# A 16-row value block of attention padded with zeros to 128 rows

## The chip, the cores and the metric

The kernel runs on one core of a Trainium2 chip. The metric is the device time of one execution in microseconds (us). The core has five engines that run their own queues and meet only at semaphores: TensorE (PE, with its weight loads shown apart as PEld), VectorE (DVE), ScalarE (ACT), GpSimd (POOL) and SyncE (SP), which issues most of the DMAs here.

## The reference

Two layers of a model of width 1024 on 512 tokens, ahead of which 16 learned meta tokens are put, so T = 528. Each layer has a feed-forward part, a mixer and a second feed-forward part. One half of the mixer is causal attention with 8 heads, query and key width 96, value width 64:

```python
h = jnp.concatenate([meta, x], axis=1)            # 16 meta tokens, then 512
for l in range(DEPTH):                            # DEPTH = 2
    h = h + 0.5 * rms_norm(swiglu(rms_norm(h, ...), ...), ...)
    z = rms_norm(h, mix_pre_g[l]) @ w_in[l]
    xr, gr, cq, ckv, kr = jnp.split(z, splits, axis=-1)
    y_lru = rglru_group(xr, gr, ...)
    y_mla = mla_group(cq, ckv, kr, ...)           # attention
    y = concat(rms_norm(y_lru), rms_norm(y_mla)) @ w_out[l]
    h = h + rms_norm(y, mix_post_g[l])
    h = h + 0.5 * rms_norm(swiglu(rms_norm(h, ...), ...), ...)
return h[:, N_META:]
# attention, per head and block of 128 queries:
s = jnp.einsum('bqhd,bkhd->bhqk', q_blk, k) * scale
s = jnp.where(kpos[None, :] <= qpos[:, None], s, -jnp.inf)
o = jnp.einsum('bhqk,bkhd->bqhd', jax.nn.softmax(s), v)
```

## The kernel before

Activations stand feature by feature: 128 features on the partitions, 528 tokens along them. Every large product is made of three matmuls per tile (high part by high part, low by high, high by low), all in fp32r; the weight tiles run through a ring of four slots that SyncE loads, ScalarE copies to the high part (`hi`, L651) and GpSimd subtracts to the low part (`lo`, L590). This fills the feed-forward parts and the projections. The order of work on every engine is the order in which its block of the program is written; there is no scheduler.

The attention of a layer (`attention`, L1627) is written as a software pipeline over 32 items: item e is head e // 4 and query block i = e % 4 + 1. A query block has 128 queries, and sees keys 0 to 16 + 128 i. The keys are taken in blocks: block 0 is the 16 meta tokens alone, blocks 1 to 4 have 128 keys each (`block_of`, L519). Round e of the loop at L1710 puts on TensorE, in this order,

- `transposes(e - 2)`: i + 1 transposes of the exponentials `prob`, 128 columns each, L1691. That of block 0 turns keys 0 to 127, not only 16;
- `scores(e)`: query by keys, all columns, and one bf16 matmul `identb` by `maskb` that adds the causal mask to the last 128 columns (L1671, L1674);
- `outputs(e - 3)`: i + 1 pairs of a weight load of `probT` and a product with the value block `vt`, added up in one PSUM region (L1702 to L1705). For block 0 only rows 0 to 15 are read of both.

Since `mm` is a helper, the trace shows scores, mask and outputs all at L1372, and they are told apart by the names of their tiles: `kt,qt`, `maskb,identb` and `vt,probT`. A fp32 matmul shows as two records, so i + 1 products with `vt` are 2 (i + 1) records; the transposes are fp32 too but show one record each.

VectorE takes the row maximum of the scores (L1300), ScalarE the exponential with its row sum (L919), and the copy of the turned exponentials from PSUM to `probT` is ScalarE's for i of 1 and 2 (L970) and VectorE's for 3 and 4 (L1293). After the four blocks of a head VectorE scales the outputs (`head_out`, L1276 and L1277).

In the first layer the 16 meta tokens are queries too, in small matmuls of 16 by 16 (`meta_scores`, `meta_transposes`, `meta_outputs`); in the last layer they are left out, as nothing reads them.

The values come from three PSUM units, of 1024, 1024 and 512 columns: five blocks of 512 (8 heads by 64). Block 0's own product runs over tokens 0 to 127, so its rows 16 to 127 hold real values of other tokens, which no one reads. ScalarE copies the three units to `vt` (L872), ahead of a weight copy `hi` (L875) and the copies to `kt`.

Of the kernel before, what the change touches and what calls it, by code (L numbers as in the profile page):

```python
# [29 lines left out]
ACT = mybir.ActivationFunctionType  # L30
AX = mybir.AxisListType

P = 128
EPS = 1e-6
LRU_C = 8.0
N_META = 16
# [11 lines left out]
VD = 64  # L48
# [19 lines left out]
    NPAR += _n  # L68


C_ID, C_ONE, C_SEL, C_MASK, C_EPS, C_LNS, NCONST = 0, P, 2 * P, 3 * P, 4 * P, 4 * P + 1, 4 * P + 2


S_XR, S_CQ, S_GATE, S_CKV, S_KR, S_GR, S_V, S_K, S_Q, S_OUT = 0, 4, 7, 8, 10, 11, 15, 16, 17, 21
# [27 lines left out]
def build_program(nc, a, out, depth, d_ff):  # L102
# [64 lines left out]
    def slot_used(n):  # L167

        return n + 1 + RING
# [41 lines left out]
    with ExitStack() as ctx:  # L211
# [31 lines left out]
        consts = sb("consts", [P, NCONST], F32)  # L243
# [31 lines left out]
        vt = over("vt", [P, 5, HEADS * VD], F32, xch_at)  # L275
# [18 lines left out]
        probT = [over(f"probT{i}", [P, 5 * P], F32, z_at + 4 * CH + i * 5 * P * 4) for i in range(3)]  # L294
# [24 lines left out]
        def pair(i):  # L319
            return ps[:, i * 1024:(i + 1) * 1024]  # L320
# [3 lines left out]
        sel = consts[:, C_SEL:C_SEL + P]  # L324
        eps = consts[:, C_EPS:C_EPS + 1]
        ln_scale = consts[:, C_LNS:C_LNS + 1]

        def col(name, l, k, p=P):
            c = PCOL[name] + k
            return par[0:p, l, c:c + 1]  # L330
# [55 lines left out]
        psum_free = [sem(f"psum_free{i}") for i in range(4)]  # L386
# [132 lines left out]
        def block_of(j):  # L519

            return (0, N_META) if j == 0 else (N_META + (j - 1) * P, P)
# [109 lines left out]
        def _(act):  # L631
# [102 lines left out]
            def seam(b):  # L734
# [23 lines left out]
                if b < NB:  # L758
# [7 lines left out]
                                 scale=-1.0).then_inc(setup_exp, 1)  # L766
# [32 lines left out]
            def mixer(b):  # L799
# [10 lines left out]
                for g, dst in enumerate((rg, ig)):  # L810
                    for c in range(WC):
                        u = U[b, "gate"] + WC * g + c
# [3 lines left out]
                        else:  # L816
                            act.wait_ge(slots_used, slot_used(s0 + S_GATE))
                        nc.scalar.activation(halves(dst[:, c, :], False), unit(u, False), ACT.Tanh,
                                             scale=0.5, bias=half_b[:, l, g, c:c + 1])\
                            .then_inc(psum_free[pair_of(u)], 1)  # L820
                    hi(s0 + 10 + g)
                for c in range(QC):
                    u = U[b, "cq"] + c
                    act.wait_ge(psum_free[pair_of(u)], read_out(u))
                    nc.scalar.activation(cqh[:, c, :], cq[:, c, :], ACT.Copy,
                                         scale=col("mla_q_norm_g", l, c)).then_inc(cqh_ready, 1)

                for c in range(WC):
                    u = U[b, "gate"] + c
# [14 lines left out]
                for c in range(KVC):  # L844
                    act.wait_ge(ckvn_ready, KVC * l + c + 1)
                    nc.scalar.activation(ckvh[:, c, :], ckv[:, c, :], ACT.Copy,
                                         scale=col("mla_kv_norm_g", l, c)).then_inc(ckvh_ready, 1)
# [7 lines left out]
                for c in range(WC):  # L855
                    u = U[b, "gr"] + c
# [4 lines left out]
                u = U[b, "sel"]  # L861
                nc.scalar.activation(halves(tmp[0], False), unit(u, False), ACT.Copy)\
                    .then_inc(psum_free[pair_of(u)], 1)
                for i in range(3):
                    u = U[b, "v"] + i

                    if i < 2:
                        act.wait_ge(v_mm, 2 * l + i + 1)
                    else:
                        act.wait_ge(slots_used, slot_used(s0 + S_V))  # L870
                    n = 2 if i < 2 else 1
                    nc.scalar.activation(vt[:, 2 * i:2 * i + n, :],  # L872
                                         pair(pair_of(u)).rearrange("p (a b) -> p a b", a=2)[:, 0:n, :],
                                         ACT.Copy).then_inc(psum_free[pair_of(u)], 1)
                hi(s0 + 19)  # L875
                for i in range(HEADS // 2):
                    u = U[b, "k"] + i
# [16 lines left out]
                for c in range(WC):  # L894
                    act.wait_ge(yn_ready, WC * l + c + 1)
                    nc.scalar.activation(ylh[:, c, :], xc[:, c, :], ACT.Copy,
                                         scale=col("lru_out_g", l, c)).then_inc(ylh_ready, 1)
# [10 lines left out]
                for e in range(ITEMS + 2):  # L908
                    if e >= 2 and copied_by_act((e - 2) % NQ + 1):
                        transposed_copy_act(l, e - 2)  # L910
                    if e < ITEMS:
                        E, i = ITEMS * l + e, e % NQ + 1
# [12 lines left out]
                    i = e - (ITEMS - NQ)  # L925
# [18 lines left out]
                for i in range(NQ):  # L944
# [4 lines left out]
                                                scale=1.0 / W, bias=eps))  # L949
                nc.scalar.activation(small[:, 32:36], small[:, 32:36], ACT.Exp, scale=-0.5)\  # L950
                    .then_inc(rs_att, 1)
                for c in range(WC):
                    act.wait_ge(tr_mm, WC * l + c + 1)
                    pr, g = pair(pair_of(U[b, "tr"] + c)), col("mla_out_g", l, c)
                    if not trimmed(b):
                        nc.scalar.activation(xh[:, WC + c, 0:N_META], pr[:, 512:512 + N_META], ACT.Copy,
                                             scale=g)
# [402 lines left out]
        def _(pe):  # L1360
# [10 lines left out]
            def mm(o, w, x, start, stop):  # L1371
                return nc.tensor.matmul(o, w, x, start=start, stop=stop)  # L1372
# [254 lines left out]
            def attention(b):  # L1627
                l = b // 3

                last = U[b, "tr"] - 1  # L1630
                for u in range(last - 3, last + 1):
                    pe.wait_ge(psum_free[pair_of(u)], read_out(u))
                pe.wait_ge(krope_ready, 2 * (l + 1))
                m0, nm = n_meta_layers(l), N_META

                def meta_scores():
                    for hd in range(HEADS):
                        o = meta_turned(hd * nm, nm)  # L1640
                        mm(o, qt(hd)[:, 0:nm], kt(hd)[:, 0:nm], True, False)
                        ins = mm(o, identb[0:nm, 0:nm], maskb[0:nm, 0:nm], False, True)
                    ins.then_inc(s0_mm, 1)

                def meta_transposes():
                    pe.wait_ge(s0_exp, m0 + 1)
                    for hd in range(HEADS):

                        ins = mm(meta_turned(hd * nm, nm), prob[3][0:nm, hd * nm:(hd + 1) * nm],
                                 ident[0:nm, 0:nm], True, True)  # L1650
                    ins.then_inc(t0_mm, 1)

                def meta_outputs():
                    pe.wait_ge(t0_copied, 2 * m0 + 1)
                    for hd in range(HEADS):
                        ins = mm(ps[0:nm, 7 * 512 + hd * VD:7 * 512 + (hd + 1) * VD],
                                 probT[2][0:nm, hd * nm:(hd + 1) * nm],
                                 vt[0:nm, 0, hd * VD:(hd + 1) * VD], True, True)
                    ins.then_inc(o0_mm, 1)

                def scores(e):
                    E, hd, i = ITEMS * l + e, e // NQ, e % NQ + 1
                    t0, nk, c = block_of(i)[0], keys_of(i), place(e)
                    if before(e) is not None:
                        copied(before(e))
                    elif e == NQ and not trimmed(b):
                        pe.wait_ge(t0_copied, 2 * m0 + 1)
                    parts = [(0, nk, c)] if i < NQ else [(0, HALF, c), (HALF, HALF, c + 512)]
                    for k0, n, c0 in parts:
                        tail = k0 + n == nk  # L1670
                        mm(ps[:, c0:c0 + n], qt(hd)[:, t0:t0 + P], kt(hd)[:, k0:k0 + n], True, not tail)  # L1671
                        if tail:

                            ins = mm(ps[:, c0 + n - P:c0 + n], identb[:, :], maskb[:, :], False, True)  # L1674
                    ins.then_inc(s_mm, 1)

                def copied(e):

                    full, i = ITEMS // 2 * l + e // NQ * 2, e % NQ + 1
                    if copied_by_act(i):  # L1680
                        pe.wait_ge(t_act, full + i)
                    else:
                        pe.wait_ge(t_dve, full + i - 2)

                def transposes(e):
                    E, i = ITEMS * l + e, e % NQ + 1
                    pe.wait_ge(prob_ready, E + 1)
                    for j in range(i + 1):

                        k0, c0 = block_of(j)[0], place(e) + j * P  # L1690
                        ins = nc.tensor.transpose(ps[:, c0:c0 + P], prob[e % 4][:, k0:k0 + P], ident)  # L1691
                    ins.then_inc(t_mm, 1)

                def outputs(e):
                    hd, i = e // NQ, e % NQ + 1
                    copied(e)
                    if i == 1 and hd >= 2:
                        pe.wait_ge(o_copied, HEADS * l + hd - 1)
                    if e == NQ and not trimmed(b):
                        pe.wait_ge(t0_copied, 2 * m0 + 2)  # L1700
                    c0 = (hd % 2) * 512 + (i - 1) * VD
                    for j in range(i + 1):  # L1702
                        kn = block_of(j)[1]
                        ins = mm(pair(3)[:, c0:c0 + VD], probT[e % 3][0:kn, j * P:(j + 1) * P],
                                 vt[0:kn, j, hd * VD:(hd + 1) * VD], j == 0, j == i)  # L1705
                    ins.then_inc(pv_mm, 1)

                if not trimmed(b):
                    meta_scores()
                for e in range(ITEMS + 3):  # L1710
                    if e == 2 and not trimmed(b):
                        meta_transposes()
                    if 2 <= e < ITEMS + 2:
                        transposes(e - 2)
                    if e < ITEMS:
                        scores(e)
                    if e == 3 and not trimmed(b):
                        meta_outputs()
                    if e >= 3:
                        outputs(e - 3)  # L1720
# [36 lines left out]
def _consts():  # L1757
    c = np.zeros((P, NCONST), np.float32)
    c[:, C_ID:C_ID + P] = np.eye(P)
    c[:, C_ONE:C_ONE + P] = 1.0  # L1760
    for i in range(ROPE):
        for q in range(P // ROPE):
            c[i, C_SEL + q * ROPE + i] = 1.0
            c[ROPE + i, C_SEL + q * ROPE + i] = 1.0
    c[:, C_MASK:C_MASK + P] = np.triu(np.full((P, P), MASKED), 1)
    c[:, C_EPS] = EPS
    c[:, C_LNS] = -0.5 * np.log(NOPE + ROPE)
    return c

# [57 lines left out]
```

## Time and profile before

| | us |
|---|---|
| median of 3 executions | 2104.96 |
| lowest, highest | 2102.6, 2106.19 |
| the profiled execution | 2107.37 |
| its span, first to last instruction | 2105.5 |
| mean granted TensorE clock in it | 0.991 |

The span is 1.9 us shorter than its execution. In the rows below a line of a timeline gives the start in us, the time that the merged instructions cover, the engine, the line of the program, the operation, its output and inputs, their shapes, how many instructions are merged, and in brackets how long the engine sat idle before, and what ended that. `issue` stands for an idle time for which the profile shows nothing waited for. A shape such as `16*128` of a weight load is rows by columns of what is loaded into the array.

### The profile page before, as it was taken

The numbers are of one execution on the slowest core, as the hardware profiler recorded it, in microseconds if no ns is written. First come the engines' busy times: TensorE is split into PE (matmuls) and PEld (weight loads), VectorE is DVE, ScalarE is ACT, GpSimd is POOL, SyncE is SP. The second block draws the span as 40 slices with busy tenths as digits, with TensorE's granted clock in tenths as the row PEclk, the third lists the DMA queues.
The fourth block names the chain that finished last, engine by engine and source line by source line (L and its number), as shares of the span: only waits on it lengthen the run. The fifth ranks groups of instructions, "written<-read, shape, count | busy, mean of one in ns | idle before, by whom it ended". The sixth has DMA issues, their size and how long they took to land.

```text
span 2105.5 us, 39769 instructions
## 1 busy us (share of the span) xinstructions
PE 2062.0 (98%) x16488; PEld 2013.7 (96%) x16488; DVE 726.6 (35%) x1070; ACT 767.4 (36%) x1189; POOL 1057.1 (50%) x1280
## 2 busy tenths in 40 slices
PE   9999999999999999999999999999999999999998
PEld 8999999989889999999999999999898889999997
DVE  5222210468544322220062222104785453222102
ACT  5322232446545322332252222324455453332321
POOL 6655554566205655554375555545662156555542
PEclk9999999999999999999999999999999999999999
DMA  3222322122102222232222323221221013333322
GB/s 138 90 90 90 93 97 96 55 93 79 41 14 69 93 89 89 89 108 84 70 90 90 90 90 93 97 94 58 96 76 41 30 54 109 99 91 91 105 97 68
DMA packets 48274, 174.91 MB, mean 83 GB/s; under 512 B 5168, under 2 KB 9392, under 8 KB 48176
## 3 DMA queue, kind: packets, MB, share of 16 engines
q1 hardware_dynamic: 45792, 170.97, 25.6%
q10 hardware_dynamic: 2384, 2.52, 0.4%
q8 instruction: 75, 1.23, 0.2%
q14 instruction: 23, 0.19, 0.0%
HBM read 171.37 MB, written 2.10 MB: 82 GB/s over the span
## 4 chain that ended last, share of the span: by engine, by line
PE 85%; DVE 9%; POOL 2%; issue 2%; ACT 1%; DMA 1%; POOLq 0%; ACTq 0%; DVEq 0%; SPq 0%
PE ps L1372 83%; DVE xl L1046 2%; POOL wlo L590 1%; DVE h L1041 1%; PE ps L1691 1%; DVE xc L1137 1%; POOL tmp L623 1%; DVE tmp L1035 1%; DVE xcl L1145 0%; DVE ig L1158 0%; DVE xc L1160 0%; DVE cql L1152 0%; ACT xh L675 0%; DVE rg L1161 0%; DVE xc L1134 0%
## 5 line engine op out<-in xcount | busy, mean ns | idle before, releaser
L590 POOL TENSOR_TENSOR wlo<-raw,whi 128x256 fp32r<-128x256 f32 (+2 forms) x1192 | 991.1, 863 | 930.1 <-ACT whi L651 930.0
L1372 PE MATMUL ps<-xh,whi 128*128 128x264 f32 (+1 forms) x3392 | 727.3, 287 | 23.9 <-DVE xl L1046 18.0
L1372 PE MATMUL ps<-xl,whi 128*128 128x264 f32 (+1 forms) x3392 | 716.8, 284 | 0.0
L1372 PE MATMUL ps<-xh,wlo 128*128 128x264 f32 (+1 forms) x3392 | 716.0, 284 | 0.0
L1372 PEld LDWEIGHTS ps<-xh,whi 128*128 128x128 f32 x3392 | 538.7, 189 | 34.8 <-DVE xl L1046 24.0
L651 ACT ACTIVATE whi<-raw 128x1024 fp32r<-128x1024 f32 (+2 forms) x298 | 334.0, 1122 | 564.7 <-DMA raw<-in_ffn_down 263.1
L1372 PEld LDWEIGHTS ps<-xl,whi 128*128 128x128 f32 x3392 | 538.0, 189 | 0.8
L1372 PEld LDWEIGHTS ps<-xh,wlo 128*128 128x128 f32 x3392 | 537.5, 189 | 0.0
L1372 PE MATMUL ps<-hidh,whi 128*128 128x264 f32 (+1 forms) x1408 | 314.1, 284 | 0.0
L1372 PE MATMUL ps<-hidl,whi 128*128 128x264 f32 (+1 forms) x1408 | 312.9, 283 | 0.0
L1372 PE MATMUL ps<-hidh,wlo 128*128 128x264 f32 (+1 forms) x1408 | 312.9, 283 | 0.0
L1372 PEld LDWEIGHTS ps<-hidl,whi 128*128 128x128 f32 x1408 | 229.8, 188 | 0.1
L1372 PEld LDWEIGHTS ps<-hidh,wlo 128*128 128x128 f32 x1408 | 229.5, 188 | 0.0
L1372 PEld LDWEIGHTS ps<-hidh,whi 128*128 128x128 f32 x1408 | 229.0, 188 | 0.1
L1096 DVE TENSOR_TENSOR tmp<-ps,rs_in 128x528 f32<-128x528 f32 (+1 forms) x88 | 61.9, 704 | 407.4 <-PE ps L1372 407.4
L1075 DVE TENSOR_TENSOR tmp<-tmp,tmp 128x528 f32<-128x528 f32 (+3 forms) x44 | 42.0, 954 | 421.9 <-ACT tmp L706 387.2
L782 ACT ACTIVATE hidh<-tmp 128x528 f32 (+3 forms) x88 | 56.5, 642 | 228.6 <-DVE tmp L1100 228.6
L1093 DVE TENSOR_TENSOR tmp<-ps,rs_in 128x528 f32<-128x528 f32 (+1 forms) x88 | 61.9, 703 | 205.3 <-PE ps L1372 192.0
L779 ACT ACTIVATE tmp<-tmp 128x528 f32<-128x528 f32 (+1 forms) x88 | 56.6, 643 | 166.3 <-DVE tmp L1093 166.2
L1103 DVE TENSOR_TENSOR hidl<-tmp,hidh 128x528 f32 (+3 forms) x88 | 69.9, 794 | 80.6 <-ACT hidh L782 80.6
L623 POOL TENSOR_TENSOR tmp<-tmp,tmp 128x264 f32<-128x264 f32 (+1 forms) x66 | 52.6, 796 | 80.5 <-ACT tmp L680 76.7
L1046 DVE SCALAR_TENSOR_TENSOR xl<-h,par,xh 128x264 fp32r<-128x264 f32 (+1 forms) x96 | 76.5, 810 | 20.7 <-ACT xh L675 20.5
(174 smaller groups left out, 1556.0 us busy)
## 6 DMA issues: line engine op xcount, KB each, us to landing
raw<-in_ffn_gate SPq DMA_DIRECT2D x88, 512.0 KB, 3.5
raw<-in_ffn_up SPq DMA_DIRECT2D x88, 512.0 KB, 3.5
raw<-in_ffn_down SPq DMA_DIRECT2D x64, 704.0 KB, 4.0
raw<-in_w_in SPq DMA_DIRECT2D x28, 512.0 KB, 3.6
raw<-in_w_out SPq DMA_DIRECT2D x16, 512.0 KB, 3.5
raw<-in_w_q SPq DMA_DIRECT2D x8, 384.0 KB, 3.1
out_t<-h SPq DMA_DIRECT2D x16, 128.0 KB, 1.7
h<-in_x ACTq DMA_DIRECT2D x2, 528.0 KB, 8.5
```

The source lines that it names most:

```text
L590: ins = nc.gpsimd.tensor_tensor(wlo[:, r, at], raw[:, r, at], whi[:, r, at].bitcast(F32), ALU.subtract)
L623: nc.gpsimd.tensor_tensor(hs, hs, square_of(k, s, trim), ALU.add)\
L651: nc.scalar.activation(whi[:, r, 0:k], raw[:, r, 0:k], ACT.Copy).then_inc(hi_ready, 1)
L779: nc.scalar.activation(toks(tmp[2], trim), toks(tmp[0], trim), ACT.Silu).then_inc(silu_ready, 1)
L782: nc.scalar.activation(toks(hidh[:, mm, :], trim), toks(tmp[3], trim), ACT.Copy).then_inc(hidh_ready, 1)
L1035: nc.vector.tensor_tensor(scratch(k, s), half(f(b - 1, k), trim, s), bank(U[b, "post"], trim, s), ALU.mult).then_inc(step_ready, 1)
L1046: nc.vector.scalar_tensor_tensor(half(xl[:, k, :], trim, s), half(h[:, k, :], trim, s), col(g, l, k), half(xh[:, k, :], trim, s).bitcast(F32),
L1075: nc.vector.tensor_tensor(acc, acc, part(tmp[m % 2], trim), ALU.add).then_inc(sum_ready, 1)
L1093: nc.vector.tensor_tensor(halves(tmp[0], trim), unit(ug, trim), halves(rs_in, trim), ALU.mult).then_inc(psum_free[pair_of(ug)], 1)
L1096: nc.vector.tensor_tensor(halves(tmp[1], trim), unit(uu, trim), halves(rs_in, trim), ALU.mult).then_inc(psum_free[pair_of(uu)], 1)
L1103: nc.vector.tensor_tensor(toks(hidl[:, mm, :], trim), toks(tmp[3], trim), toks(hidh[:, mm, :], trim).bitcast(F32), ALU.subtract).then_inc( ...
L1372: return nc.tensor.matmul(o, w, x, start=start, stop=stop)
```

## The change

The copy of the first value unit is split in two. Block 0 is multiplied, on its way out of PSUM, by a new constant column that is 1 on rows 0 to 15 and 0 below; block 1 is copied as before. The products for block 0 then run over all 128 rows of `probT` and `vt`. The turned exponentials of keys 16 to 127 meet rows of zeros there, and these keys are counted once, in block 1, as before. The number and the order of TensorE's instructions stay as they are; ScalarE has one more instruction per layer. The small matmuls of the meta queries still read 16 rows.

```diff
+C_ID, C_ONE, C_SEL, C_MASK, C_EPS, C_LNS, C_META, NCONST = (
+    0, P, 2 * P, 3 * P, 4 * P, 4 * P + 1, 4 * P + 2, 4 * P + 3)
...
+        is_meta = consts[:, C_META:C_META + 1]
...
+                    if i == 0:
+                        nc.scalar.activation(vt[:, 0, :], pair(pair_of(u))[:, 0:512], ACT.Copy, scale=is_meta)
+                        nc.scalar.activation(vt[:, 1, :], pair(pair_of(u))[:, 512:1024],
+                                             ACT.Copy).then_inc(psum_free[pair_of(u)], 1)
+                        continue
                     n = 2 if i < 2 else 1
                     nc.scalar.activation(vt[:, 2 * i:2 * i + n, :],
...
                     for j in range(i + 1):
-                        kn = block_of(j)[1]
-                        ins = mm(pair(3)[:, c0:c0 + VD], probT[e % 3][0:kn, j * P:(j + 1) * P],
-                                 vt[0:kn, j, hd * VD:(hd + 1) * VD], j == 0, j == i)
+                        ins = mm(pair(3)[:, c0:c0 + VD], probT[e % 3][:, j * P:(j + 1) * P],
+                                 vt[:, j, hd * VD:(hd + 1) * VD], j == 0, j == i)
...
+    c[0:N_META, C_META] = 1.0
```

## Rows read from the trace of the kernel before

**Rows 1.** The page: busy time of the engines, and the chain that ended last
```profile
PE 2062.0 (98%) x16488; PEld 2013.7 (96%) x16488; DVE 726.6 (35%) x1070; ACT 767.4 (36%) x1189; POOL 1057.1 (50%) x1280
...
PE 85%; DVE 9%; POOL 2%; issue 2%; ACT 1%; DMA 1%; POOLq 0%; ACTq 0%; DVEq 0%; SPq 0%
```

**Rows 2.** Stretches: busy us of PE, PEld, DVE, ACT, POOL; granted clock; DMA share, GB/s
```profile
546.80:548.40 1.60, 1.60 (x5) 0.76 (x5) 0.00 (x0) 0.81 (x3) 1.50 (x3) 0.50 0.00 0
...
551.00:609.00 58.00, 58.00 (x402) 46.65 (x400) 28.93 (x58) 26.77 (x81) 2.78 (x4) 1.00 0.01 1
1600.00:1656.00 56.00, 56.00 (x382) 44.86 (x381) 27.55 (x55) 25.03 (x75) 4.09 (x6) 1.00 0.00 1
```

**Rows 3.** Timeline of TensorE's weight loads over one head, layer 1
```profile
559.92 0.66 PEld L1372 LDWEIGHTS ps<-vt,probT 16*128 16x128 f32 x4 [0.27 <-issue]
560.45 0.48 PEld L1691 LDWEIGHTS ps<-consts,prob 128*128 128x128 f32 x4
560.89 0.30 PEld L1372 LDWEIGHTS ps<-kt,qt 128*128 128x128 f32 x2
...
561.40 0.88 PEld L1372 LDWEIGHTS ps<-vt,probT 16*128 16x128 f32 x6 [0.17 <-issue]
565.54 1.33 PEld L1372 LDWEIGHTS ps<-vt,probT 16*128 16x128 f32 x10 [0.38 <-issue]
...
568.22 0.66 PEld L1372 LDWEIGHTS ps<-vt,probT 16*128 16x128 f32 x4 [0.27 <-issue]
```

**Rows 4.** Timeline, narrow windows: mask matmul, second 16-row load, first 128-row load
```profile
561.25 0.22 PE L1372 MATMUL ps<-maskb,identb 128*128 128x128 bf16 x1
...
561.50 0.18 PEld L1372 LDWEIGHTS ps<-vt,probT 16*128 16x128 f32 x1
...
561.76 0.19 PEld L1372 LDWEIGHTS ps<-vt,probT 128*128 128x128 f32 x1
```

**Rows 5.** Timeline, narrow window: a 128-row load right behind a mask matmul
```profile
545.35 0.19 PEld L1372 LDWEIGHTS ps<-kt,qt 128*128 128x128 f32 x1
...
545.35 0.22 PE L1372 MATMUL ps<-maskb,identb 128*128 128x128 bf16 x1
```

**Rows 6.** Groups by shape, 546 to 660 us: count, busy us and mean ns, idle before
```profile
L1372 PEld LDWEIGHTS ps<-vt,probT 128*128 128x128 f32 x160 | 20.3, 190 | 2.2
...
L1372 PEld LDWEIGHTS ps<-vt,probT 16*128 16x128 f32 x64 | 9.4, 182 | 8.2 <-issue 8.0
```

**Rows 7.** Timeline: from the scores of a head's last item to its transposes
```profile
568.33 0.71 DVE L1300 TENSOR_REDUCE small<-ps 128x1 f32<-128x528 f32 x1 [0.65 <-PE ps L1372]
...
569.67 0.19 ACT L919 ACTIVATION_READ_ACCUMULATOR prob<-ps,small 128x1 f32 x1
...
570.44 0.59 PEld L1691 LDWEIGHTS ps<-consts,prob 128*128 128x128 f32 x5
```

**Rows 8.** Timeline: the last items of layer 1's attention
```profile
609.68 0.66 PEld L1372 LDWEIGHTS ps<-vt,probT 16*128 16x128 f32 x4 [0.27 <-issue]
...
611.60 0.59 PEld L1691 LDWEIGHTS ps<-consts,prob 128*128 128x128 f32 x5
...
612.35 2.50 PEld L1372 LDWEIGHTS ps<-vt,probT 16*128 16x128 f32 x18 [0.17 <-issue]
...
612.46 0.82 DVE L1293 COPY probT<-ps 128x640 f32<-128x640 f32 x1 [0.81 <-PE ps L1691]
```

**Rows 9.** Timeline of ScalarE's value copies, the weight copy behind them, and a scaled copy's group
```profile
517.30 2.41 ACT L872 ACTIVATE vt<-ps 128x1024 f32<-128x1024 f32 x3
...
520.84 0.85 ACT L651 ACTIVATE whi<-raw 128x768 fp32r<-128x768 f32 x1 [1.13 <-DMA raw<-in_w_q]
...
L958 ACT ACTIVATE xh<-ps,par x8: 682/683/689, 620.4 to 1670.3; 128x512 fp32r<-128x512 f32 x8
```

**Rows 10.** Timeline: the 400-column score matmuls at half clock and at full clock
```profile
547.03 1.54 PE L1372 MATMUL ps<-kt,qt 128*128 128x400 f32 x2
...
606.18 0.84 PE L1372 MATMUL ps<-kt,qt 128*128 128x400 f32 x2
```

More of the change, by code:

```diff
@@ L68 @@
     NPAR += _n
-C_ID, C_ONE, C_SEL, C_MASK, C_EPS, C_LNS, NCONST = 0, P, 2 * P, 3 * P, 4 * P, 4 * P + 1, 4 * P + 2
+C_ID, C_ONE, C_SEL, C_MASK, C_EPS, C_LNS, C_META, NCONST = (
+    0, P, 2 * P, 3 * P, 4 * P, 4 * P + 1, 4 * P + 2, 4 * P + 3)
 S_XR, S_CQ, S_GATE, S_CKV, S_KR, S_GR, S_V, S_K, S_Q, S_OUT = 0, 4, 7, 8, 10, 11, 15, 16, 17, 21
```

## The prediction

> **What bounds the kernel now.** I read the page first. TensorE is busy 98% of the span, and 85% of the chain that ended last is TensorE's; no other engine is over half [rows 1]. So a change counts if it shortens TensorE's own queue, and only there. Next the windows over the two attentions, the only stages that the change touches: TensorE is busy for all of both stretches at the full clock of 2.4 GHz, VectorE for half (28.93 of 58.00 us) and ScalarE for less (26.77) [rows 2]. But "busy" hides waits here, since the modelled end of one matmul overlaps the start of the next. The weight loads show them better. Over one head each group of products with `vt` begins with a 16-row load that has an idle time of 0.17 to 0.38 us before it, ended by "issue": nothing that the profile knows of was waited for [rows 3]. Over layer 1 the 64 loads of 16 rows have 8.2 us of idle time before them, the 160 of 128 rows 2.2 us, although both kinds last about the same, 182 and 190 ns [rows 6]. It is not the load that is dear, but what stands around it.
>
> **What a switch between 16 and 128 rows costs.** Going out: two loads of one kind follow each other by 0.10 to 0.11 us. The groups of 4, 6 and 10 records cover 0.66, 0.88 and 1.33 us [rows 3], so two more records are 0.22 us. The first 128-row load, however, starts 0.26 us after the second 16-row load (561.76 less 561.50) [rows 4]. The excess is 0.15 us. Going in: the mask matmul starts at 561.25 [rows 4] and the first 16-row load at 561.40 [rows 3], 0.15 us later. Where a 128-row load follows a mask matmul, it starts in the same hundredth, at 545.35 [rows 5]. So 0.15 us there too. The rest of the idle time before a group (0.38 less 0.15 at the widest) is the streaming of the score matmuls, which stays. I read both as TensorE letting its pipeline run dry when the number of rows changes. Other readings fail on rows: a semaphore wait before the group doesn't do it, since scores also wait for a semaphore and their load follows the transposes without a gap (560.45 plus 4 by 0.11 is 560.89) [rows 3]; nor does a bf16 matmul ahead [rows 5].
>
> The Trainium skill, "TensorE: Matmul & The Clock Gate", Part 3, "The mechanism", has a rule that speaks against the change: it says that a weight load overlaps matmuls in flight only when its row group differs, and loads over all 128 rows share every group. By that rule full rows would win nothing and the sum below would be 0; the load of rows 5, which starts together with a 128-row matmul, is against it. The skill's "TensorEngine Tiling", "Key Properties", says instead that a change of tiling mode drains TensorE, without a figure; by that rule, the trace agrees, with 0.15 us a switch.
>
> **The sum.** *TensorE.* There are 32 items in each of two layers, 64 groups, and each has one switch in and one out: 128. In layer 1 the first group stands behind the 16-row matmuls of the meta queries, so it has no switch in now, and keeps one later: of 127 switches one is left, 126 go. 126 by 0.15 is 18.9 us. The products keep their count, and cost the same: pairs of 64 columns are paced by the load (0.11 us) at either number of rows [rows 3]. No trace row shows a 128-row group right behind the mask, so I bound it: a full gain by rows 5, none if it waits as the 16-row load does. I take rows 5, the nearest case.
>
> *What is late next.* A head takes 8.30 us (559.92 to 568.22) [rows 3], and would take 7.10. VectorE's and ScalarE's work in it, some half of 8.30, still fits; what may be late is latency. The tightest chain is that of the head's last scores: maximum from 568.33, then the exponential, whose sum is read from 569.67 to 569.86, and some 0.05 us to TensorE: 1.58 us [rows 7]. The transposes that need it start at 570.44, so there is 0.53 us of slack. In between lie the next group of four records, the next of six, and two switches out and one in (0.45 us), and the transposes come 0.15 us nearer by the switch in ahead of the first group, in all 0.60. The wait that appears is 0.07 us a head, in 7 heads a layer: 1.0 us. The copies to `probT` have 1.5 us of slack and lose half of it.
>
> *The end of each layer's attention.* There are no scores left to put between, so the chains bind. Counted from the group at 609.68 [rows 8]: the exponentials of the last item are ready 0.26 plus 1.58, so 1.84 us in, while TensorE could begin its transposes at 1.41. From there to the start of VectorE's copy are 0.86 us (611.60 to 612.46), the copy takes 0.82, and 0.05 us later the last group may begin, at 3.57; its ten loads end 1.15 us on, at 4.72. Now they end at 612.35 plus 2.50, 5.17 us in [rows 8]. The gain is 0.45 us where seven switches (1.05 us) were counted: 0.6 us lost a layer, 1.2 in both.
>
> *ScalarE.* The copy of the first value unit, 1024 columns, becomes two of 512. Three copies take 2.41 us now; a scaled 512-column copy from PSUM takes 0.68 [rows 9], and a plain one I put at 0.60, so 1.28 us in place of about 1.01, 0.27 more. Behind them a weight copy waits 1.13 us for its DMA anyway [rows 9], which covers that; without the cover it would be 0.27 us a layer on the way to `kt`. The PSUM pair comes free 0.27 us later too; its next user is the second key unit, a whole unit of matmuls behind, so I take nothing, and at most 0.27 us a layer, 0.5 in all, inside the range. One more column of constants and a wider read of `vt` cost nothing on any row.
>
> Sum: 18.9 less 1.0 less 1.2 is 16.7 us. The profiled execution of 2107.37 us becomes 2090.7. That execution is 2.4 us above the median of the runs shown; against the median, 2104.96 less 16.7 is **2088.3 us**, 0.8% less.
>
> Does the gain hold to the end? Ahead of the output projection TensorE has its work covered by weights that were ready long before, and everything behind is shifted as one, in a kernel whose bound is TensorE. I see nothing later that runs by another clock.
>
> **The rivals.**
> - *One side only.* The load waits at the way in for something else that stays, such as the copy it reads, or the second kind of accumulation explains the way out. For it: I know each side by itself only from neighbours. Against it: [rows 5], and the same 0.15 on both sides. 63 by 0.15 is 9.5 us, without most of the new waits: about 2096 us.
> - *Nothing.* A full-row load would wait in the same way here, or the gap moves to another place. For it: before has no 128-row group at the head of the products. Against it: the transposes follow the products without a gap, and scores the transposes [rows 3]. By the medians 2105 us. The rule of the skill named above has this result.
> - *Latency takes over earlier.* If a semaphore hop costs 0.1 us more than I read, every head loses as much: 14 by 0.1, 1.4 us. This only widens the forecast, to 2090.
> - *Slower: the clock.* In layer 1, right behind the tiny matmuls of the meta queries, the granted clock is 0.50, which is 1.2 GHz, from 546.8 to 548.4 [rows 2], and two score matmuls take 1.54 us in place of 0.84 [rows 10]. If the new rhythm of the loop, with VectorE's and ScalarE's waits put between bursts, brought TensorE to 1.2 GHz for long, a head would take 7.1 by 1.54 / 0.84, some 13.0 us, 5.9 more. From three of the sixteen heads on the gain is gone (16.7 / 5.9); one layer's eight would make 2088 plus 47, about 2135 us. Against it: both attentions run at 1.00 with the gaps that they have now [rows 2], and the change makes them denser.
>
> **How the numbers follow.** The forecast, both sides of the switch with small new waits, gets 0.80, with 2084 to 2092 as its own range: 20.5 us gained if the switches go and no wait appears, 13 if every wait is twice what I put. One side only gets 0.10, nothing 0.07, the clock 0.03. The range of 2084 to 2097 takes in the first two, less the edges. A measurement of this kernel can tell about 0.2%, 4.2 us, from no change. Both of the first two cases are faster by more than that: 0.90. Within 0.2%: 0.07. Slower: 0.03.
>
> **What would show it.** All weight loads for `vt` outside the meta queries are 128 rows; the idle time of some 8 us a layer by "issue" falls to 2 to 4; a head takes 7.1 to 7.2 us. The group of ten records spans 1.18 us and not 1.33. Transposes behind a head's last item show a wait of less than 0.1 us for ScalarE. Only one of the gaps closing would be the first rival, with a head of 7.7 us. I am wrong if the head stays near 8.3 us, if a wait of over 0.3 us a head appears on L919 or L1293, or if the granted clock in the two attentions is below 0.95.

## The result, and the profile after

The changed kernel took 2086.26 us (median of 4 executions, 2085.26 to 2089.89), the kernel before in the same comparison 2105.57 us. The ratio is 0.9907, with a 95% interval of 0.9882 to 0.9932: faster by 19 us, between 14 and 25. A later comparison of the same two kernels, told below, gave 0.9912 (0.9893 to 0.9931). The forecast was 2088.3 us. Every ratio in this document leaves out executions that took over 1.5% longer than the fastest of the same kernel.

The page after, the lines of [rows 1]: TensorE is busy 22 us less and its weight loads 9 us less; the other engines are within 4 us of before.

```profile
span 2083.4 us, 39771 instructions
...
PE 2040.0 (98%) x16488; PEld 2004.7 (96%) x16488; DVE 729.9 (35%) x1070; ACT 765.5 (37%) x1191; POOL 1057.0 (51%) x1280
...
PE 85%; DVE 9%; issue 2%; POOL 2%; ACT 1%; DMA 1%; POOLq 0%; ACTq 0%; DVEq 0%; SPq 0%
```

The weight loads of one head after, a timeline of the TensorE loads alone, to be laid beside [rows 3]. `L1379` is the helper that was L1372, and `L1698` the transposes of L1691. One row of the same view of before goes ahead of them: the load for the mask matmul that stands before the group at 561.40.

```profile
561.13 0.10 PEld L1372 LDWEIGHTS ps<-maskb,identb 128*128 128x128 bf16 x1
```

After:

```profile
562.81 0.53 PEld L1379 LDWEIGHTS ps<-vt,probT 128*128 128x128 f32 x4
563.20 0.48 PEld L1698 LDWEIGHTS ps<-consts,prob 128*128 128x128 f32 x4
563.65 0.30 PEld L1379 LDWEIGHTS ps<-kt,qt 128*128 128x128 f32 x2
563.88 0.10 PEld L1379 LDWEIGHTS ps<-maskb,identb 128*128 128x128 bf16 x1
564.00 0.75 PEld L1379 LDWEIGHTS ps<-vt,probT 128*128 128x128 f32 x6
564.65 0.56 PEld L1698 LDWEIGHTS ps<-consts,prob 128*128 128x128 f32 x5
...
567.60 1.20 PEld L1379 LDWEIGHTS ps<-vt,probT 128*128 128x128 f32 x10 [0.24 <-issue]
...
569.99 0.53 PEld L1379 LDWEIGHTS ps<-vt,probT 128*128 128x128 f32 x4
```

The groups of 4, 6 and 10 records cover 0.53, 0.75 and 1.20 us where they covered 0.66, 0.88 and 1.33: 0.13 us less each, the switch out. The brackets ahead of them are gone, or down from 0.38 to 0.24 before the group of ten: 0.14 us, the switch in. Where a bracket is gone, the starts show the same: from the mask's load to the group of six were 0.27 us (561.13 to 561.40), and are 0.12 (563.88 to 564.00), so 0.15 us less. What stays before the group of ten I read as the streaming of 400 columns of scores. A head takes 7.18 us (562.81 to 569.99), where it took 8.30.

By shape, 535 to 650 us (layer 1), the group that answers to both lines of [rows 6]:

```profile
L1379 PEld LDWEIGHTS ps<-vt,probT 128*128 128x128 f32 x224 | 27.5, 192 | 4.0 <-issue 1.7 <-DVE probT L1300 0.2
```

10.4 us of idle time before the loads of the outputs became 4.0. The loads themselves last 192 ns, where they lasted 182 (16 rows) and 190 (128 rows). The switch out is in neither figure in full: it lies between the starts of two loads of one group, where the profile shows no bracket.

To see where the whole difference sits, here are five stretches in each profile, cut at the first load of scores and at the first load of `ylh` behind each attention (us):

| profile | up to first score | attention 1 | between | attention 2 | rest | span |
|---|---|---|---|---|---|---|
| before | 543.01 | 71.76 | 980.61 | 67.00 | 443.12 | 2105.5 |
| after | 540.14 | 63.21 | 978.15 | 58.61 | 443.29 | 2083.4 |

The two attentions give 8.55 and 8.39, together 16.9 us. The other 5.2 us of the spans' difference are in stretches that the change does not touch. The second profile of the changed kernel, below, has its first score at 542.87, and three kernels whose block 0 still has 16 or 64 rows have theirs at 538.81 to 539.80, so this part is scatter from one profile to the next.

The second attention is the cleaner of the two measures. Over all profiles of kernels with one product of block 0 it takes 66.99 to 67.06 us where that product has 16 or 64 rows, and 58.60 to 58.65 where it has 96 or 128. The first attention scatters, 71.76 to 74.88 us against 62.43 to 64.88, with the time for which TensorE is at 1.2 GHz at its start: its mean granted clock is 0.98 before and 0.97 after, but 0.93 to 0.95 in the longer ones. So 8.39 us can be compared as it stands, and 8.55 within some 2 us.

### The profile page after: what moved, and what is told of

Read it like the earlier page. It is cut to its first block, busy times and chain, and to the rows that moved or that the text cites. A ratio compares the mean times of both kernels' runs of the same rounds, so it can differ in the third digit from the quotient of the medians.

```text
span 2083.4 us, 39771 instructions
## 1 busy us (share of the span) xinstructions
PE 2040.0 (98%) x16488; PEld 2004.7 (96%) x16488; DVE 729.9 (35%) x1070; ACT 765.5 (37%) x1191; POOL 1057.0 (51%) x1280
## 4 chain that ended last, share of the span: by engine, by line
PE 85%; DVE 9%; issue 2%; POOL 2%; ACT 1%; DMA 1%; POOLq 0%; ACTq 0%; DVEq 0%; SPq 0%
PE ps L1379 84%; DVE xl L1053 2%; DVE h L1048 1%; DVE xc L1144 1%; PE ps L1698 1%; POOL wlo L592 1%; DVE tmp L1042 1%; POOL tmp L625 1%; DVE xcl L1152 0%; DVE ig L1165 0%; DVE xc L1167 0%; ACT xh L677 0%; DMA h<-in_x 0%; DVE rg L1168 0%; DVE xc L1141 0%
## 5 line engine op out<-in xcount | busy, mean ns | idle before, releaser
L1379 PE MATMUL ps<-xh,whi 128*128 128x264 f32 (+1 forms) x3392 | 727.5, 287 | 23.4 <-DVE xl L1053 16.8
L1379 PE MATMUL ps<-xl,whi 128*128 128x264 f32 (+1 forms) x3392 | 716.6, 284 | 0.0
L1379 PE MATMUL ps<-xh,wlo 128*128 128x264 f32 (+1 forms) x3392 | 715.9, 284 | 0.0
L1379 PEld LDWEIGHTS ps<-xh,whi 128*128 128x128 f32 x3392 | 538.6, 189 | 34.2 <-DVE xl L1053 22.0
L1379 PEld LDWEIGHTS ps<-xl,whi 128*128 128x128 f32 x3392 | 538.0, 189 | 0.7
L1379 PEld LDWEIGHTS ps<-xh,wlo 128*128 128x128 f32 x3392 | 537.4, 189 | 0.0
L1379 PE MATMUL ps<-hidh,whi 128*128 128x264 f32 (+1 forms) x1408 | 314.1, 284 | 0.0
L1379 PE MATMUL ps<-hidl,whi 128*128 128x264 f32 (+1 forms) x1408 | 312.9, 283 | 0.0
L1379 PE MATMUL ps<-hidh,wlo 128*128 128x264 f32 (+1 forms) x1408 | 312.8, 283 | 0.0
L1379 PEld LDWEIGHTS ps<-hidl,whi 128*128 128x128 f32 x1408 | 229.8, 188 | 0.1
L1379 PEld LDWEIGHTS ps<-hidh,wlo 128*128 128x128 f32 x1408 | 229.5, 188 | 0.0
L1379 PEld LDWEIGHTS ps<-hidh,whi 128*128 128x128 f32 x1408 | 229.0, 188 | 0.1
L1107 DVE TENSOR_TENSOR tmp<-tmp,tmp 128x528 f32<-128x528 f32 (+1 forms) x88 | 80.9, 919 | 13.6 <-ACT tmp L781 3.0
```

The costliest lines, as they stand in the source:

```text
L1107: nc.vector.tensor_tensor(toks(tmp[3], trim), toks(tmp[2], trim), toks(tmp[1], trim), ALU.mult).then_inc(hid_ready, 1)
```

## Experiments

Theory A, at the start: TensorE lets its pipeline run dry whenever the number of rows that it works on changes between two modes of the array, about 0.15 us each time, and the whole gain is the 126 such switches that go. The rivals were that ScalarE's half of the change takes part, that the price belongs to small loads as such, that it is paid once a group, and that it depends on what stands ahead.

### ScalarE's half alone

```diff
 (the changed kernel, with)
+                        kn = N_META if j == 0 else P
-                        ins = mm(..., probT[e % 3][:, j * P:(j + 1) * P], vt[:, j, ...], j == 0, j == i)
+                        ins = mm(..., probT[e % 3][0:kn, j * P:(j + 1) * P], vt[0:kn, j, ...], j == 0, j == i)
```

> ScalarE's half of the change alone: the zero rows are written, but block 0 is still multiplied over 16 rows. My theory: all of the gain is TensorE's, and the 0.27 us a layer that the split copy costs lies under the weight copy's DMA wait (1.13 us before). Time as before within 0.2% (2101 to 2110 us), a head at 8.30 us. Rival (ScalarE's part costs or gains something by itself, for instance through the key copies behind it): off by over 1 us a layer.

2105.08 us against 2105.56, ratio 0.9995 (0.9970 to 1.0019). The timeline of its ScalarE, the rows that answer to [rows 9]:

```profile
513.22 0.67 ACT L874 ACTIVATE vt<-ps,consts 128x512 f32<-128x512 f32 x1
513.79 0.59 ACT L875 ACTIVATE vt<-ps 128x512 f32<-128x512 f32 x1
514.26 1.52 ACT L879 ACTIVATE vt<-ps 128x1024 f32<-128x1024 f32 x2
516.96 0.85 ACT L653 ACTIVATE whi<-raw 128x768 fp32r<-128x768 f32 x1 [1.18 <-DMA raw<-in_w_q]
```

The value copies cover 2.56 us (513.22 to 515.78) and not 2.41, and the weight copy behind them still waits 1.18 us for its DMA. The split costs 0.15 us, not the 0.27 forecast (neighbouring copies overlap at their ends), and it is hidden. Its attentions take 72.86 (at a mean granted clock of 0.95) and 66.99 us: no gain without the full rows.

### TensorE's half alone

```diff
 (the kernel before, with the change at L1702 to L1705 and L872 left as it was)
```

> TensorE's half of the change alone: block 0 over 128 rows, but the value copy as before. Leaves out the zeroing, so keys 16 to 127 are counted twice. My theory: head 7.18 us, both attentions together 16.9 us shorter than before, as in the changed kernel within 0.3 us. Rival (the split copy moves something before attention, where the profile of after is 2.9 us ahead already at the first score): this kernel doesn't show that lead.

One execution, 2084.8 us. Attentions 63.21 and 58.60 us, as after (63.21 and 58.61) within 0.01 us; the first score is at 539.65, so the lead before attention has nothing to do with the split copy. The gain in the attentions is TensorE's alone.

### How many rows count as full

```diff
 (the changed kernel, with kn = 64, or kn = 96, in place of N_META above)
```

> As the changed kernel, but block 0 is multiplied over 64 rows. Theory A (a switch costs 0.15 us whenever the tiling mode of the array changes, and 64 rows are another mode than 128): as before, head 8.30 us, about 2105 us. Theory B (the cost belongs to loads of 32 rows or fewer): as after, head 7.18 us, about 2088 us.

> As the changed kernel, but block 0 is multiplied over 96 rows. Theory A (the mode changes; 96 rows fit only the full array): as after, head 7.18 us, about 2088 us. Theory C (any load of fewer than 128 rows next to full ones makes the pipeline run dry): as before, head 8.30 us, about 2105 us.

Loads of the products by shape, 535 to 650 us, first 64 rows, then 96:

```profile
L1379 PEld LDWEIGHTS ps<-vt,probT 64*128 64x128 f32 x64 | 9.4, 184 | 8.2 <-issue 8.0
```

```profile
L1379 PEld LDWEIGHTS ps<-vt,probT 96*128 96x128 f32 x64 | 9.7, 191 | 3.9 <-issue 1.7 <-DVE probT L1300 0.2
```

64 rows behave as 16 did, with the same 8.2 us idle as in [rows 6]; 96 rows behave as 128. Times: 2102.28 us (ratio 0.9977, 0.9959 to 0.9995) and 2087.21 us (0.9897, 0.9857 to 0.9938). The second attention takes 67.06 and 58.60 us; the first takes 73.09 and 64.88, both at a mean granted clock of 0.95. This is theory A: the price is gone somewhere between 64 and 96 rows, and it is no smaller for 64 rows than for 16. In every one of these kernels the load and the product change their rows together, so which of the two the price belongs to stays open. The Trainium skill, "TensorEngine Tiling", "Available Configurations", lists 32, 64 and 128 rows as the modes; 96 fit only the last, and by that rule, the trace agrees. The 3 us by which the 64-row kernel lies under before are not explained by its attentions, which are 1.4 us longer than before in its profile.

### Twice as many switches

The product of block 0 is made a second time behind the others: once over 16 rows in the kernel before, once over 128 in the changed one.

```diff
-                    for j in range(i + 1):
+                    order = list(range(i + 1)) + [0]
+                    for q, j in enumerate(order):
...
-                                 vt[0:kn, j, hd * VD:(hd + 1) * VD], j == 0, j == i)
+                                 vt[0:kn, j, hd * VD:(hd + 1) * VD], q == 0, q == i + 1)
```

> The kernel before, with block 0's product over 16 rows made a second time behind the others of each group, so the number of switches between 16 and 128 rows doubles. Counts the meta tokens twice, so its output is another. My theory: per group 2 records more, 0.21 us, and one switch in and one out more, 0.30 us: 64 by 0.51 is 33 us, so about 2138 us, a head at 10.3 us. Rival (the price is paid once for each group, for its first load, whatever stands ahead): 64 by 0.21 is 14 us, about 2119 us, a head at 9.2 us.

> The changed kernel with the same second product of block 0, over 128 rows: 2 records more a group and no switch. Counts the meta tokens twice, so its output is another. Both theories: 64 by 0.21 is 13.7 us over the changed kernel, less up to 1 us because the longer head gives the exponential of its last item time: about 2100 us, a head at 8.0 us. The difference between the two kernels with a second product is 36 us by my theory, 19 us by the rival.

Full rows: 2100.3 us (ratio to before 0.9970, 0.9951 to 0.9990), 13.2 above the changed kernel in the same comparison (2087.06), as 64 groups by 0.21 say; none of its ten executions is over 2103.64 us. 16 rows: six executions at 2141.2, 2142.5, 2143.9, 2201.7, 2202.3 and 2261.9 us, against 2104.2 before. The three lowest give a ratio of 1.0179 (1.0148 to 1.0210). That is 42 us over its twin with full rows, where four switches a group by 0.15 us should give 38 less the small waits. The forecast of 2138 is missed by 4 us, and nothing forecast the three high times. The profile was of the highest one, and its stretches (busy us of PE, PEld, DVE, ACT, POOL, then granted clock) show where the time went:

```profile
500.00:540.00 40.00, 39.12 (x285) 36.81 (x283) 31.88 (x37) 27.02 (x39) 22.55 (x26) 1.00 0.27 80
...
560.00:600.00 40.00, 40.00 (x138) 30.23 (x136) 8.68 (x17) 7.68 (x23) 0.00 (x0) 0.50 0.00 0
600.00:660.00 60.00, 60.00 (x207) 45.98 (x206) 12.76 (x26) 10.68 (x31) 0.00 (x0) 0.50 0.00 1
```

From 560 us on TensorE runs at 0.50, that is 1.2 GHz, to the end of the attention, which takes 148.1 us; the second takes 143.7. The first attention of the next kernel, the same code, took 89.4 us. That is an extra of about 59 us, which fits the levels: 2142, one attention slow 2202, both 2262. The mean clocks fit too: 0.987 to 0.989 in the three lowest, 0.958 and 0.959 in the two at 2202, 0.930 in the highest. The twin with full rows has as many products and not one such execution in ten, so it is the switches, and not the added work, that go with the loss of the clock. By what means is not shown.

### The same once more, at full clock

> The kernel with the second 16-row product again (counts the meta tokens twice), for a profile in which its attentions run at full clock; the last one had TensorE at 1.2 GHz through both. Theory: at full clock a head takes 10.3 to 10.8 us and the clean runs' 2142 us is 9 us above the 2132 that two further switches of 0.15 us would give on top of 2104 and 13.7, so one of the four switches is dearer: the one in behind a 64-column product, at 0.2 to 0.3 us. Rival: the excess is clock, not switches, and the granted clock in the attentions is below 0.97.

One execution, 2167.07 us, and a mixed profile. In layer 1 the clock is 1.00 from 560 to 620 us. Its loads there:

```profile
576.02 1.69 PEld L1372 LDWEIGHTS ps<-vt,probT 16*128 16x128 f32 x12 [0.38 <-issue]
...
586.33 1.69 PEld L1372 LDWEIGHTS ps<-vt,probT 16*128 16x128 f32 x12 [0.38 <-issue]
```

A head takes 10.31 us. Its twin with full rows takes 8.07 (570.08 to 578.15 by its loads). 2.24 us for 16 switches is 0.14 each, so none of the four in a group is dear, and my expectation of one at 0.2 to 0.3 us was wrong. The clock falls twice: at the end of the first attention, for some 10 us, and between 1650 and 1670 us, in the middle of the second, where it stays down:

```profile
620.00:640.00 20.00, 20.00 (x112) 17.80 (x110) 7.56 (x15) 4.77 (x19) 0.00 (x0) 0.74 0.00 1
...
1630.00:1650.00 20.00, 20.00 (x125) 15.64 (x124) 7.67 (x16) 6.48 (x20) 0.00 (x0) 1.00 0.00 1
1650.00:1670.00 20.00, 20.00 (x94) 15.64 (x95) 5.48 (x12) 5.54 (x16) 0.00 (x0) 0.72 0.00 1
1670.00:1690.00 20.00, 20.00 (x69) 14.94 (x68) 4.11 (x9) 3.40 (x10) 0.00 (x0) 0.50 0.00 0
```

The rhythm of the loop was the same before the second fall as in the heads that ran at full clock: the last whole head, from 1641.81 to 1652.11 by its loads, takes 10.30 us. So with twice the switches the same code may keep the clock or lose it. A short stretch like the first is also the likely reason for the 4 us over 2138: 20 us at a mean of 0.74 cost some 5 us, and the three lowest executions have a mean clock of 0.987 to 0.989 where before has 0.991. No profile was taken of one of them, so this is argued and not shown.

### Block 0 last

```diff
-                    for j in range(i + 1):
+                    order = list(range(1, i + 1)) + [0]
+                    for q, j in enumerate(order):
```

> The kernel before with block 0's 16-row product last in its group and not first: the same work and as many switches, but the switch in stands behind a 64-column product and no longer behind the mask matmul, the switch out ahead of the transposes. If a switch in costs 0.15 us wherever it stands: 2105 us, a head at 8.3 us. If it is dearer behind a product (0.2 to 0.3 us, as the kernel with the second product suggests): 64 by 0.05 to 0.15, 3 to 10 us more, 2108 to 2115 us.

2103.79 us against 2103.81, ratio 0.9988 (0.9966 to 1.0010). Two groups of four records in layer 1, one head apart, in its timeline of loads:

```profile
568.00 0.66 PEld L1372 LDWEIGHTS ps<-vt,probT 128*128 128x128 f32 x4
...
576.30 0.66 PEld L1372 LDWEIGHTS ps<-vt,probT 128*128 128x128 f32 x4
```

8.30 us, as before, and the second attention takes 67.00 us, as before. A pair of switches costs the same behind a mask matmul, behind a 64-column product and ahead of a transpose. The first attention takes 74.88 us. Its granted clock falls twice at the start, the second time behind the output matmuls of the meta queries:

```profile
552.00:556.00 4.00, 4.00 (x18) 3.38 (x18) 2.06 (x4) 1.05 (x4) 2.31 (x4) 0.57 0.00 0
```

### Full rows in two more places, and the changed kernel again

```diff
+                    chain.link(nc.vector.memset(osb0[:, :], 0.0))
...
-                        nc.tensor.transpose(pr[:, 512:512 + N_META], osb0[0:N_META, c * P:(c + 1) * P],
-                                            ident[0:N_META, 0:N_META])
+                        mm(pr[:, 512:512 + N_META], osb0[:, c * P:(c + 1) * P], ident[:, 0:N_META], True, True)
...
-                        ins = mm(o, identb[0:nm, 0:nm], maskb[0:nm, 0:nm], False, True)
+                        ins = mm(o, identb[:, 0:nm], maskb[:, 0:nm], False, True)
```

> The changed kernel once more, beside the next one and for the scatter of profiles. Time 2086 to 2088 us. If the 5 us by which the profiles of before and after differ outside of attention are scatter, the first score stands anywhere from 538.8 to 543 us, and the two attentions together at 121.8 us within 1.7 us (the clock behind the meta queries' matmuls).

> The changed kernel, with full rows also for the mask matmuls of the meta queries (128 rows of the identity and the mask, in which rows 16 to 127 add zero) and for the four small transposes of their outputs (the array that they read is filled with zeros first). 16 switches in the mask part, 8 around the transposes. My theory: the four transposes lose 4 by 0.30 less 0.1 for a second record each, some 0.8 us; the mask part loses little, as its matmuls of 16 columns drain fast and TensorE waits for the exponentials right behind. 0.8 to 2 us below the changed kernel, 2085 to 2087 us, not told from no change by the times. Rival (each of the 24 switches costs 0.15 us on the path): 3.6 us less.

The changed kernel again: 2087.06 us, ratio 0.9912 (0.9893 to 0.9931). Its attentions take 63.49 and 58.65 us, 122.1 together, as expected; the first score is at 542.87 and the span 2087.2, 3.8 us over the first profile of the same kernel. So the first-score time moves by 2.7 us with nothing changed.

With more full rows: 2084.77 us, ratio 0.9901 (0.9881 to 0.9920), the lowest of all that compute the reference. The two sets of six executions overlap (2085.6 to 2089.2 and 2082.4 to 2086.8), so the 2.3 us by which it is ahead are likely but small. Its loads from the first score of a meta query to the first of an ordinary item:

```profile
539.45 0.13 PEld L1380 LDWEIGHTS ps<-kt,qt 128*16 128x16 f32 x2 [1.21 <-issue]
539.50 0.09 PEld L1380 LDWEIGHTS ps<-maskb,identb 128*16 128x16 bf16 x1
...
540.15 0.30 PEld L1380 LDWEIGHTS ps<-kt,qt 128*128 128x128 f32 x2
```

and the same places in the changed kernel's first profile:

```profile
540.14 0.13 PEld L1379 LDWEIGHTS ps<-kt,qt 128*16 128x16 f32 x2 [1.20 <-issue]
540.30 0.08 PEld L1379 LDWEIGHTS ps<-maskb,identb 16*16 16x16 bf16 x1
...
542.12 0.30 PEld L1379 LDWEIGHTS ps<-kt,qt 128*128 128x128 f32 x2
```

0.70 us in place of 1.98: the mask part, of which I had said that it loses little, gives 1.28 us for its 16 switches, 0.08 each. The attention as a whole is only 0.8 to 1.1 us shorter (62.43), since TensorE then waits for the exponentials. The part with the small transposes, from the first load of `ylh` to the first of `xh`, takes 8.55 us where it took 8.82: 0.3, not the 0.8 that I had put there. The sum came out in the range of 0.8 to 2, its two terms the wrong way round; the rival's 3.6 us did not come.

## Why the prediction was right

**The bound.** That only TensorE's own queue counts held: ScalarE's half alone does nothing, TensorE's half alone does everything.

**The price of a switch.** 0.15 us on each side was the central term. By the profile after it is 0.13 to 0.14 out and 0.14 to 0.15 in for the groups read above, by the kernel with doubled switches 0.14. That TensorE's pipeline runs dry is the reading of this delay; the rows show the delay and not the emptying. The 126 switches at 0.15 made 18.9 us. The one step that no row of before showed, a 128-row group right behind a mask matmul, went the way of [rows 5]: matmul and load start in the same hundredth, at 564.00 in that head and at 598.71 in the last one of the layer.

```profile
598.71 0.22 PE L1379 MATMUL ps<-maskb,identb 128*128 128x128 bf16 x1
598.71 0.53 PEld L1379 LDWEIGHTS ps<-vt,probT 128*128 128x128 f32 x4
```

The rivals of one side only (a head of 7.7 us) and of nothing (8.3 us) are out with a head of 7.18, and with them the rule weighed there from the Trainium skill, "TensorE: Matmul & The Clock Gate", Part 3, that a weight load overlaps running matmuls only when its row group differs: the head of 7.18 us speaks against it.

**What is late next.** A head was put at 8.30 less 1.20 plus 0.07, 7.17 us. VectorE's and ScalarE's rows of that chain after, for comparison with [rows 7]:

```profile
563.07 0.71 DVE L1307 TENSOR_REDUCE small<-ps 128x1 f32<-128x528 f32 x1 [0.64 <-PE ps L1379]
563.81 0.70 ACT L926 ACTIVATE prob<-ps,small 128x528 f32<-128x528 f32 x1 [1.20 <-DVE small L1307]
564.41 0.19 ACT L926 ACTIVATION_READ_ACCUMULATOR prob<-ps,small 128x1 f32 x1
```

1.58 us from 563.07 end at 564.65, and at 564.65 the transposes begin. The slack of 0.53 us is used up, as the sum had it, and the wait is so short that it has no bracket. From the start of the group of six to the transposes are 0.65 us, where its six loads at 0.10 to 0.11 us would take 0.61: a wait of some 0.04 us, where 0.07 was forecast. The copies to `probT`, said to lose half of their 1.5 us of slack, keep 1.1 (the copy that ends at 564.65 is read from 565.75 on).

**The end of an attention.** Forecast from the group at 0: transposes at 1.84, last group at 3.57, its end at 4.72. After, from the group at 598.71:

```profile
600.55 0.53 PEld L1698 LDWEIGHTS ps<-consts,prob 128*128 128x128 f32 x5 [0.26 <-ACT prob L926]
...
601.36 0.82 DVE L1300 COPY probT<-ps 128x640 f32<-128x640 f32 x1 [0.81 <-PE ps L1698]
...
602.24 1.19 PEld L1379 LDWEIGHTS ps<-vt,probT 128*128 128x128 f32 x10 [0.21 <-DVE probT L1300]
```

1.84, 3.53 and 4.72 us. Both waits that were forecast are there, by name, 0.26 and 0.21 us.

**The sum.** 16.7 us forecast, 16.9 measured in the two attentions. By layer the terms give 8.2 (62 switches) and 8.5 (64), and 8.55 and 8.39 were measured. The second of these is clean; the first holds the scatter of the clock, so that the totals agree to 0.2 us is in part luck. The medians differ by 19.3 us in the first comparison and 17.2 in the second, which had more executions; both intervals hold 16.7. What the profiles of the first comparison show beyond 16.9 lies elsewhere and did not repeat. The bounds of the forecast's own range do not follow from its terms: with no wait at all they give 18.9 us and not 20.5, and with every wait doubled 14.5 and not 13.

**ScalarE.** The step "0.27 us more" was too high, 0.15 by the row; its cover held, so nothing hung on it.

**The slower rival.** The clock did not fall in the changed kernel: 1.00 over most of both attentions, in a table of stretches for comparison with [rows 2].

```profile
544.60:545.80 1.20, 1.20 (x3) 0.42 (x3) 0.00 (x0) 0.46 (x2) 0.82 (x2) 0.50 0.00 0
548.00:598.00 50.00, 50.00 (x398) 44.51 (x396) 28.93 (x58) 25.59 (x79) 2.77 (x4) 1.00 0.01 2
1587.00:1634.00 47.00, 47.00 (x368) 41.63 (x368) 26.73 (x54) 22.95 (x71) 3.24 (x4) 1.00 0.01 1
```

The short fall behind the meta queries' matmuls stays. But the mechanism is real in this loop, in the other direction: with more switches, not with fewer. I had given it a price of 47 us for one attention, and it was about 60. The prediction took waits of the other engines between bursts for the danger; what went with the fall was more switches, in a loop without new waits.

## What to carry to other kernels

A matmul over few rows between matmuls over 128 costs two switches, here 0.28 to 0.30 us a pair (0.17 between matmuls of 16 columns). The trace books the switch in as idle time before a weight load that ended by "issue", and the switch out only as a longer step between two loads, while the engine's busy share stays at 100%. Where the operand can be padded with zeros at no cost, 96 rows were as good as 128 here, and 64 as bad as 16; nothing between 64 and 96 was tried. Before a gain of this kind is counted whole, follow the latency chain to the next wait: in the forecast it took 2.2 of 18.9 us.

## What the runs showed that was not expected

The clock can be lost in a stage in which TensorE counts as 100% busy. With twice the switches TensorE ran at 1.2 GHz in five of the fourteen attentions of seven executions (one of them from its middle on), if the levels of the times are read as above. In one of the two profiles the clock fell in mid-stage, without any wait that was new.

The kernel before may be near that edge too. In the three later comparisons 8 of its 48 executions near 2104 us are at 2115 to 2120 us instead, with a mean clock of 0.983 to 0.986, and none of the 31 executions of kernels whose block 0 has 96 or 128 rows shows the like. One kernel with 16 rows had such an execution too (2119.55 us); two others with as many switches had none in ten each. None of these executions was profiled, so I leave it open where their clock fell and whether the change also removes this.
